# A block's first projection with the high-half passes ahead of the low-half passes, and the wait for the low half between them

## The chip, the cores and the metric

The kernel runs on one core of a Trainium2 chip. The metric is the device time of the whole program in microseconds (us). Engines are named as in the profile: PE is TensorE (PEld its weight loads), DVE is VectorE, ACT is ScalarE, POOL is GpSimd, SP issues the DMAs.

## The reference

Two layers, each over 2048 prompt rows and 32 sample rows of width 1024. A layer normalises its input, projects it once for all head groups, runs sparse attention (A), a gated linear recurrence (B) and retention (C), gates each group and projects back. Cut to what matters:

```python
def mixer_layer(x, pos, k_past, v_past, ik_past, s_hgrn, s_ret, lb, norm_g, w_in, ...):
    h = rms_norm(x, norm_g)
    proj = jnp.einsum('btd,dn->btn', h, w_in)
    (aq, ak, av, ag, iq, ik, iw, bq, bf, bi, bg, cq, ck, cv, cg) = jnp.split(proj, SPLIT_IDX, axis=-1)
    aq = rope(rms_norm(aq.reshape(b, t, A_HEADS, HEAD_DIM), q_norm_g), pos)
    ...
    ya = sparse_attention(aq, iq, iw * IDX_W_SCALE, pos, k_all, v_all, ik_all) * jax.nn.silu(ag)
    ...
    s_hgrn_new, ob = chunked_scan(gla_chunk, ...)
    ...
    s_ret_new, oc = chunked_scan(ret_chunk, s_ret.astype(f32), (cq, ck, cv))
    ...
    y = jnp.concatenate([ya, yb.astype(ya.dtype), yc.astype(ya.dtype)], axis=-1)
    out = x + jnp.einsum('btm,md->btd', y, w_out)
```

The change touches the `proj` product alone. It is computed in near-f32 precision from f16 halves: h = high + low, w = high + low, and the sum high x high + high x low + low x high is accumulated in f32.

## The kernel before

**Layers.** Each layer has two halves, one after the other. `recurrent_half` normalises and projects the rows, runs both recurrences, and writes queries, keys and gates to DRAM. `attention_half` reads them back, searches the top keys, attends and projects out. In between all engines meet.

**Blocks.** The recurrent half walks over 17 blocks of rows: blocks 0 to 15 of 128 prompt rows, and block 16 with the 32 sample rows. Block 0 is written out, blocks 1 to 14 are a hardware loop of seven passes with two blocks in each, and blocks 15 and 16 are written out again. Every engine has its own program in this form, so each has a back edge after blocks 2, 4, ..., 12. What one engine needs of another it waits for by semaphore, in the fixed order of its own program.

**The projection.** The 3912 output columns are eight groups in the order `bqf`, `big`, `cqk`, `cvg`, `iq`, `kvi`, `aq`, `ag` (`GI` is a group's place in it, 0 for `bqf`). `project` (L345) computes one group into one bank of PSUM (`PJ`, four banks in turn): for each of the `DC` = 8 chunks of 128 input columns, three matmuls, with the transposed input as stationary operand and 512 columns of weights as the moving one. L362 is high input by high weights, L363 high input by low weights, L364 low input by high weights. That is 24 matmuls for a group and 192 for a block.

**Where the input comes from.** The transposed input of block t + 1 is made during block t. ACT rounds the normalised rows to f16 (`xh`), DVE takes the remainder (`xl`, L840). In the middle of the last group `ag` of block t, after 5 of its 8 chunks, PE transposes both (`x_transposes`, L342) into two PSUM banks. ACT copies the first bank to `hTh` (L483, semaphore `hTh_ok`), and DVE copies the second to `hTl` (L845, semaphore `hTl_ok`). Nine matmuls of `ag` are still to come on PE then. DVE's copy stands in its program behind the norm of `aq`: L813 and L815 on `sqa`, of which L813 waits for POOL's `rsa`. ACT has only the gate of `ag` behind its copy.

**The start of a block.** PE's `block_of` waits for both semaphores, then projects `bqf`, transposes the rotated queries of the block before (`qrp`, which DVE finishes at L650), projects `big`, and transposes `bqf`, which ACT has copied. From these ACT makes `ef` (L503), and DVE's work on the new block begins with it at L699. Ahead of that DVE still ends the old block: the rotation of `aq` into `qrp`, the output of retention, the gate `ga`, and `ql`, the low half of the queries (L831).

**Block 0** has one thing more to wait for: the f16 halves of the weights. ACT rounds them (`w_in_hi`, L470), and DVE (L854) and, for three chunks in each of the groups 2 to 6, POOL (L610, L612) make the low halves (`w_in_lo`). At `t == 0` every `project` waits for all low weights of its group (L359).

Of the kernel before, what the change touches and what calls it, by code (L numbers as in the profile page):

```python
# [75 lines left out]
def build(nc, xin, cache_k, cache_v, cache_i, st_h, st_r, norm_g, w_in, q_g, k_g, lb_logits, h_g, r_g, w_out,  # L76
# [3 lines left out]
    DC = D // P  # L80
# [24 lines left out]
    def recurrent_half(l, sem):  # L105

        with ExitStack() as ctx:
            def sb(name, shape, dt=F32):
                return ctx.enter_context(nc.sbuf_tensor(f"{name}_{l}", shape, dt))


            wh, wl = sb("w_in_hi", [P, DC * N_IN], F16), sb("w_in_lo", [P, DC * N_IN], F16)
# [13 lines left out]
            hTh, hTl = sb("hTh", [P, 2, DC, P], F16), sb("hTl", [P, 2, DC, P], F16)  # L126
# [33 lines left out]
            def ps(name):  # L160
# [14 lines left out]
            x_sq, x_ms, x_rs, xh_ok, xl_ok, xT_ok, hTh_ok, hTl_ok = (sem(n) for n in (  # L175
                "x_sq", "x_ms", "x_rs", "xh_ok", "xl_ok", "xT_ok", "hTh_ok", "hTl_ok"))
# [21 lines left out]
            def weights(g, c, half):  # L198

                n0, wd = DC * GOFF[GROUPS[g][0]] + c * GROUPS[g][1], GROUPS[g][1]  # L200
                return half[:, n0:n0 + wd]
# [125 lines left out]
            def _(pe):  # L327
                mm = nc.tensor.matmul
# [16 lines left out]
                def project(t, T, par, n, c0=0, c1=DC):  # L345

                    g = GI[n]
                    wd = GROUPS[g][1]
                    if c0 > 0:
                        pass  # L350
                    elif not isinstance(t, int) or t > 0 or g >= PJ_BANKS:
                        pn = GROUPS[(g - PJ_BANKS) % NG][0]
                        tt = t if g >= PJ_BANKS else t - 1
                        if pn in ACT_G:
                            pe.wait_ge(act_read, tt * len(ACT_G) + ACT_G[pn])
                        if pn in DVE_G:
                            pe.wait_ge(dve_read, tt * len(DVE_G) + DVE_G[pn])
                    if isinstance(t, int) and t == 0:
                        pe.wait_ge(w_lo_ok[g], DC)  # L359
                    out = PJ[g % PJ_BANKS][0:T, 0:wd]  # L360
                    for c in range(c0, c1):
                        mm(out, hTh[:, par, c, 0:T], weights(g, c, wh), start=(c == 0), stop=False)  # L362
                        mm(out, hTh[:, par, c, 0:T], weights(g, c, wl), start=False, stop=False)  # L363
                        last = mm(out, hTl[:, par, c, 0:T], weights(g, c, wh), start=False, stop=(c == DC - 1))  # L364
                    if c1 == DC:
                        last.then_inc(proj, 1)

                def block_of(t, T, par):
                    pe.wait_ge(hTh_ok, t + 1)
                    pe.wait_ge(hTl_ok, t + 1)  # L370
                    project(t, T, par, "bqf")
                    if not isinstance(t, int) or t > 0:
                        query_transposes(t - 1, P)
                    project(t, T, par, "big")
                    pe.wait_ge(act_read, t * len(ACT_G) + ACT_G["bqf"])
                    transposes(trv[0], [bqf[0:T, c, :] for c in range(4)], T).then_inc(bqfT_ok, 1)
                    project(t, T, par, "cqk")
                    project(t, T, par, "cvg")
                    project(t, T, par, "iq")
# [5 lines left out]
                    for p in range(2):  # L385
                        last = nc.tensor.transpose(TR[0][0:T, p * P:(p + 1) * P], k2T[:, p, 0:T], ident[:])
# [4 lines left out]
                    for p in range(2):  # L391
                        for i in reversed(range(T // WIN)):
                            m = (WIN, 2 * WIN, P, P)[i]
                            q = qe if i == 0 else qw
                            for h in range(2):
                                r = slice(64 * h, 64 * h + 64)
                                last = mm((ATT, OU)[h][0:m, p * P + i * WIN:p * P + (i + 1) * WIN], kt[r, p, i, 0:m],
                                          q[r, p, i * WIN:(i + 1) * WIN], start=True, stop=True)
# [9 lines left out]
                    for p in range(2):  # L408
                        for h in range(2):
                            r = slice(64 * h, 64 * h + 64)  # L410
                            last = mm((ATT, TR[0])[h][0:T, p * P:p * P + T], cqkT[r, 2 + p, 0:T], cqkT[r, p, 0:T],
                                      start=True, stop=True)
# [10 lines left out]
                    for c, s in enumerate((akh[:, 0:P], akh[:, P:2 * P], akl[:, 0:P], akl[:, P:2 * P])):  # L423
                        last = nc.tensor.transpose(trh[0][:, c, 0:T], s[0:T, :], identh[0:T, 0:T])
# [23 lines left out]
                pe.wait_ge(prep, 1)  # L448
                x_transposes(0)
                block_of(0, P, 0)  # L450
                if NB > 2:
                    with pe.Fori(1, NB - 1, 2) as t:
                        block_of(t, P, 1)
                        block_of(t + 1, P, 0)
# [1191 lines left out]
    with ExitStack() as whole:  # L1646
        def sem(name):
            return whole.enter_context(nc.semaphore(name))
# [151 lines left out]
```

## Time and profile before

| | us |
|---|---|
| median of 3 runs | 4125.5 (4125.13 to 4126.38) |
| the profiled execution | 4124.83 |
| its span in the trace | 4123.0 |
| recurrent half, layer 0 / layer 1: first matmul | 14.0 / 2072.1 |
| attention half, layer 0 / layer 1: first matmul | 940.3 / 2998.5 |
| PE busy over the span | 3622.0 (88%) |
| DVE / ACT / POOL busy | 2644.5 / 2336.1 / 1070.5 |
| L362, L363, L364: matmuls each | 2176 |

The three lines of `project` are the dearest on PE, 814 + 812 + 811 us by the sum of their durations. A matmul of 512 columns lasts about 0.38 us in the records and the next one begins about 0.22 us after it, so they overlap, and what a stream of them costs is read from the starts. A row of the order of time names in brackets how long the engine was idle before it and which instruction released it.

### The profile page before, as it was taken

To read this page: it belongs to the slowest core of one execution; us is meant where nothing else is said; L and a number is where in the kernel's file an instruction comes from. 1 tells how busy PE (TensorE), PEld (TensorE's weight loads), DVE (VectorE), ACT (ScalarE), POOL (GpSimd) and SP (SyncE) were. 2 spreads that over 40 slices of the span, in tenths; PEclk is the share of its full clock that TensorE was granted. 3 is DMA by queue.
4 is the path that set the end of the run, shared out by engine and by line. 5 is a ranking of instruction groups with operands and counts; after the bars stand their busy time and mean duration, and the time that the engine had idled before them with its cause. 6 is when DMAs were issued, how large, how long until landed. Compare 5 with 4: busy or idle time off the path is not lost. (4 is left out here: it accounts for less than half of the span.)

```text
span 4123.0 us, 57079 instructions
## 1 busy us (share of the span) xinstructions
PE 3622.0 (88%) x17620; PEld 1694.0 (41%) x17620; DVE 2644.5 (64%) x6138; ACT 2336.1 (57%) x4386; POOL 1070.5 (26%) x1772
## 2 busy tenths in 40 slices
PE   5999999985888889889859999999858888898897
PEld 2555555541333323243325555555413333233443
DVE  6666666656676766656266666666566767666562
ACT  5333333326779888777253333333267798887772
POOL 4110010004533332333040001010055333323330
PEclk8999999996889999989979999999968899999899
DMA  5111111115200000001151111111152000000010
GB/s 179 37 39 37 37 37 40 38 28 145 80 33 32 21 22 26 15 28 35 37 178 39 37 36 37 39 38 38 27 144 82 30 33 21 22 26 15 28 35 38
DMA packets 168514, 194.54 MB, mean 47 GB/s; under 512 B 76576, under 2 KB 114464, under 8 KB 168288
## 3 DMA queue, kind: packets, MB, share of 16 engines
q1 hardware_dynamic: 168288, 192.01, 15.2%
q8 instruction: 83, 1.36, 0.1%
q14 instruction: 143, 1.17, 0.1%
HBM read 130.57 MB, written 61.36 MB: 47 GB/s over the span
## 5 line engine op out<-in xcount | busy, mean ns | idle before, releaser
L1441 ACT ACTIVATE signs<-sc,mid 128x640 bf16<-128x640 f32 (+14 forms) x720 | 974.8, 1355 | 251.7 <-POOL mid L1497 234.7
L362 PE MATMUL PJ<-w_in_hi,hTh 128*128 128x512 f16 (+2 forms) x2176 | 813.8, 374 | 69.6 <-DVE hTl L845 34.7
L363 PE MATMUL PJ<-w_in_lo,hTh 128*128 128x512 f16 (+2 forms) x2176 | 812.3, 373 | 0.0
L364 PE MATMUL PJ<-w_in_hi,hTl 128*128 128x512 f16 (+2 forms) x2176 | 811.1, 373 | 0.0
L1346 PE MATMUL PV<-pt,va_p 128*65 128x512 f32 x1088 | 583.8, 624 | 77.2 <-ACT pt L1421 71.0
L1589 DVE SCALAR_TENSOR_TENSOR sc<-rl,iwb,sc 128x512 f32<-128x512 f32 (+5 forms) x602 | 416.3, 709 | 287.3 <-ACT rl L1412 279.2
L1494 POOL TENSOR_SCALAR dlt<-cnta,stp 128x1 f32<-128x1 f32 (+1 forms) x720 | 274.5, 381 | 1137.4 <-ACT signs L1441 1135.5
L1497 POOL TENSOR_SCALAR mid<-mid,dlt,stp 128x1 f32<-128x1 f32 (+1 forms) x720 | 434.8, 604 | 75.6
L1526 DVE CUSTOM_DVE_ANT_0 junkb<-AX,mneg 128x512 bf16<-128x512 f32 (+5 forms) x720 | 412.3, 601 | 39.6 <-PE AX L1291 32.5
L1421 ACT ACTIVATE pt<-LG 128x512 f32<-128x512 f32 (+1 forms) x612 | 330.6, 554 | 141.7 <-PE LG L1331 123.6
L1412 ACT ACTIVATE rl<-AX 128x512 f32<-128x512 f32 (+5 forms) x688 | 345.3, 530 | 105.9 <-PE AX L1304 79.6
L362 PEld LDWEIGHTS PJ<-w_in_hi,hTh 128*128 128x128 f16 (+1 forms) x2176 | 214.4, 99 | 305.7 <-issue 73.8
L364 PEld LDWEIGHTS PJ<-w_in_hi,hTl 128*128 128x128 f16 (+1 forms) x2176 | 214.8, 99 | 241.3 <-issue 7.5
L1303 PE MATMUL AX<-key2h_p,iq 128*128 128x512 f16 (+3 forms) x608 | 238.8, 396 | 79.0 <-ACT rl L1412 59.9
L363 PEld LDWEIGHTS PJ<-w_in_lo,hTh 128*128 128x128 f16 (+1 forms) x2176 | 214.6, 99 | 211.5 <-issue 5.5
L596 POOL TENSOR_TENSOR rsx<-ssx,mhalf 128x1 f32<-128x1 f32 x34 | 19.0, 558 | 958.5 <-DVE ssx L835 958.5
L1304 PE MATMUL AX<-key2l_p,iq 128*128 128x512 f16 (+3 forms) x608 | 238.0, 395 | 0.0
L1331 PE MATMUL LG<-identb,mneg 128*128 128x512 bf16 (+1 forms) x612 | 237.2, 388 | 0.0
L1346 PEld LDWEIGHTS PV<-pt,va_p 128*65 128x65 f32 x1088 | 144.7, 142 | 219.1 <-ACT pt L1421 96.3
L1384 PE MATMUL X<-w_out_hi,yTh 128*128 128x512 f16 (+1 forms) x544 | 208.9, 384 | 11.3 <-DVE yTl L1564 7.4
L1572 DVE SCALAR_TENSOR_TENSOR xr<-X,xr 128x512 f32<-128x512 f32 (+1 forms) x68 | 46.9, 690 | 261.3 <-PE X L1386 261.2
L1385 PE MATMUL X<-w_out_lo,yTh 128*128 128x512 f16 (+1 forms) x544 | 208.6, 384 | 0.0
(268 smaller groups left out, 5885.9 us busy)
## 6 DMA issues: line engine op xcount, KB each, us to landing
yt<-y_d SPq DMA_DIRECT2D x32, 512.0 KB, 3.5
out<-xr SPq DMA_DIRECT2D x32, 512.0 KB, 2.6
w_in_hi<-in SPq DMA_DIRECT2D x40, 256.0 KB, 4.9
w_stage<-in SPq DMA_DIRECT2D x40, 256.0 KB, 3.9
x<-in SPq DMA_DIRECT2D x16, 512.0 KB, 3.8
w_in_lo<-in SPq DMA_DIRECT2D x32, 256.0 KB, 6.4
y_d<-ga SPq DMA_DIRECT2D x32, 256.0 KB, 2.0
q<-q_d SPq DMA_DIRECT2D x32, 256.0 KB, 2.8
```

What stands on the lines that cost most here:

```text
L362: mm(out, hTh[:, par, c, 0:T], weights(g, c, wh), start=(c == 0), stop=False)
L363: mm(out, hTh[:, par, c, 0:T], weights(g, c, wl), start=False, stop=False)
L364: last = mm(out, hTl[:, par, c, 0:T], weights(g, c, wh), start=False, stop=(c == DC - 1))
L1303: mm(ps[0:T, 0:wd], q, keys[c][2][0][:, c0:c0 + wd], start=True, stop=False)
L1346: mm(PV[0:HD + 1, 0:4 * T], va[c][0:kw, k0 // P, kv, :], pt[0:kw, (n - 1) % 3, 0:4 * T], start=(k0 == 0), stop=(k0 + kw == keys_of(j)[1])) ...
L1412: A(rl[0:T, (n - 1) % 3, 0:wd], ax_bank("idx", j, k)[0:T, 0:wd], ACT.Relu).then_inc(s["relu_ok"], 1)
L1421: A(pt[0:kw, (n - 1) % 3, 0:4 * T], LG[(n - 1) % 3][0:kw, 0:4 * T], ACT.Exp, scale=HD ** -0.5).then_inc(s["exp_ok"], 1)
L1441: A(signs[p][0:T, 0:W], sc[u % 3][0:T, 0:W], ACT.Sign, scale=-1.0, bias=small[u % 3]["mid"][0:T, :], accum_out=small[u % 3]["cnta"][0:T, : ...
L1494: G.tensor_scalar(v["dlt"], v["cnta"], float(W - 2 * K), stp[0:T, u % 3, i:i + 1], ALU.is_le, ALU.mult).then_inc(s[f"dlt_ok{p}"], 1)
L1497: G.tensor_scalar(v["mid"], v["mid"], v["dlt"], stp[0:T, u % 3, i + 1:i + 2], ALU.add, ALU.subtract).then_inc(s[f"mid_ok{p}"], 1)
L1526: V.tensor_tensor_reduce(out=junk[0:T, n % 2, 0:wd], in0=ax_bank("qk", j, k)[0:T, 0:wd], in1=mneg[j % 3][0:T, c0:c0 + wd], scale=1.0, scal ...
L1589: V.scalar_tensor_tensor(out=o, in0=src, scalar=w1, in1=o, op0=ALU.mult, op1=ALU.add).then_inc(s["acc_ok"], 1)
```

## The change

Group 0 (`bqf`) alone is affected. Its loop over the chunks now has the two passes with `hTh` only; after it comes the wait for `hTl_ok`, and then the eight passes with `hTl` in a loop of their own. The wait for `hTl_ok` at the head of `block_of` is gone. The other seven groups keep their three passes chunk by chunk.

```diff
@@ -361,13 +361,17 @@
                     for c in range(c0, c1):
                         mm(out, hTh[:, par, c, 0:T], weights(g, c, wh), start=(c == 0), stop=False)
                         mm(out, hTh[:, par, c, 0:T], weights(g, c, wl), start=False, stop=False)
-                        last = mm(out, hTl[:, par, c, 0:T], weights(g, c, wh), start=False, stop=(c == DC - 1))
+                        if g > 0:
+                            last = mm(out, hTl[:, par, c, 0:T], weights(g, c, wh), start=False, stop=(c == DC - 1))
+                    if g == 0:
+                        pe.wait_ge(hTl_ok, t + 1)
+                        for c in range(DC):
+                            last = mm(out, hTl[:, par, c, 0:T], weights(g, c, wh), start=False, stop=(c == DC - 1))
                     if c1 == DC:
                         last.then_inc(proj, 1)
 
                 def block_of(t, T, par):
                     pe.wait_ge(hTh_ok, t + 1)
-                    pe.wait_ge(hTl_ok, t + 1)
                     project(t, T, par, "bqf")
```

On PE, at the back edge of the loop, before (the end of `ag` of one block, the branch, and `bqf` of the next; names in brackets are the semaphores waited for):

```order
L364 MATMUL PJ_0<-w_in_hi,hTl 128x512
L452 REGISTER_ALU
L452 COMPARE_AND_BRANCH
L362 MATMUL PJ_0<-w_in_hi,hTh 128x512 [waits dve_read,hTl_ok,hTh_ok]
L363 MATMUL PJ_0<-w_in_lo,hTh 128x512
L364 MATMUL PJ_0<-w_in_hi,hTl 128x512
...
L333 MATMUL ATT<-ident,qrp 128x128 [waits aq_ok]
```

and the same place now (L365 is what was L364 in the groups after the first, L369 the new loop, L456 the old L452):

```order
L365 MATMUL PJ_0<-w_in_hi,hTl 128x512
L456 REGISTER_ALU
L456 COMPARE_AND_BRANCH
L362 MATMUL PJ_0<-w_in_hi,hTh 128x512 [waits dve_read,hTh_ok]
L363 MATMUL PJ_0<-w_in_lo,hTh 128x512
...
L369 MATMUL PJ_0<-w_in_hi,hTl 128x512 [waits hTl_ok]
L369 MATMUL PJ_0<-w_in_hi,hTl 128x512 x7
L333 MATMUL ATT<-ident,qrp 128x128 [waits aq_ok]
```

The wait for `hTl_ok` moved from the first of the 24 matmuls to the 17th, and the eight matmuls that read `hTl` moved behind the sixteen that don't.

On PE, in block 0, before (the transposes of x, then `bqf`):

```order
L342 MATMUL TR_0<-identh,xl 128x128 [waits xl_ok]
L342 MATMUL TR_0<-identh,xl 128x128 x7
L362 MATMUL PJ_0<-w_in_hi,hTh 128x512 [waits w_lo_ok0,hTl_ok,hTh_ok]
...
L362 MATMUL PJ_0<-w_in_hi,hTh 128x512 [waits w_lo_ok1]
```

and now:

```order
L342 MATMUL TR_0<-identh,xl 128x128 [waits xl_ok]
L342 MATMUL TR_0<-identh,xl 128x128 x7
L362 MATMUL PJ_0<-w_in_hi,hTh 128x512 [waits w_lo_ok0,hTh_ok]
...
L369 MATMUL PJ_0<-w_in_hi,hTl 128x512 [waits hTl_ok]
L369 MATMUL PJ_0<-w_in_hi,hTl 128x512 x7
L362 MATMUL PJ_0<-w_in_hi,hTh 128x512 [waits w_lo_ok1]
```

The wait for the low weights of group 0 stays at the head; the one for those of group 1 (`w_lo_ok1`, at `big`) stays where it was.

## Rows read from the trace of the kernel before

**Rows 1.** Costliest groups: line, engine, operation, count | busy, mean ns | idle before, releaser.

```profile
L362 PE MATMUL PJ<-w_in_hi,hTh 128*128 128x512 f16 (+2 forms) x2176 | 813.8, 374 | 69.6 <-DVE hTl L845 34.7
```

**Rows 2.** By stretch: stretch, length, busy PE, PEld, DVE, ACT, POOL; clock, DMA share, GB/s.

```profile
71.00:900.00 829.00, 797.04 (x4855) 448.06 (x4856) 555.19 (x1380) 278.32 (x652) 88.17 (x87) 0.99 0.14 40
```

**Rows 3.** Waits of PE, 117 to 910, then 2177 to 2970: total, times, longest.

```profile
PE PJ L362 <- DVE hTl L845: 12.8, 14, 0.9
PE PJ L362 <- issue: 1.2, 2, 0.8
...
PE PJ L362 <- DVE hTl L845: 12.0, 13, 0.9
```

**Rows 4.** Order of time, start of block 3: start, duration, instruction [idle before <-releaser].

```profile
214.94 0.61 PE L342 MATMUL TR<-identh,xl 128*128 128x128 f16 x8
215.14 1.02 ACT L483 ACTIVATE hTh<-TR 128x1024 f16<-128x1024 f16 x1 [1.15 <-PE TR L342]
...
217.12 0.38 PE L364 MATMUL PJ<-w_in_hi,hTl 128*128 128x512 f16 x1
...
217.47 0.69 DVE L845 COPY hTl<-TR 128x1024 f16<-128x1024 f16 x1
...
218.42 0.39 PE L362 MATMUL PJ<-w_in_hi,hTh 128*128 128x512 f16 x1 [0.92 <-DVE hTl L845]
```

**Rows 5.** Order of time: start of block 16 in layer 0, of block 1 in layer 1.

```profile
869.96 0.69 DVE L845 COPY hTl<-TR 128x1024 f16<-128x1024 f16 x1
...
870.75 0.38 PE L362 MATMUL PJ<-w_in_hi,hTh 128*32 128x512 f16 x1 [0.46 <-issue]
...
2175.92 0.69 DVE L845 COPY hTl<-TR 128x1024 f16<-128x1024 f16 x1 [0.47 <-PE TR L342]
...
2177.03 0.38 PE L364 MATMUL PJ<-w_in_hi,hTl 128*128 128x512 f16 x1
...
2177.24 0.38 PE L362 MATMUL PJ<-w_in_hi,hTh 128*128 128x512 f16 x1
```

**Rows 6.** Order of time behind the start of block 3; then DVE's waits, 117 to 900.

```profile
220.18 0.42 DVE L650 TENSOR_TENSOR qrp<-rt 128x256 f32<-128x256 f32 x1
...
223.60 0.60 PE L333 MATMUL ATT<-ident,qrp 128*128 128x128 f32 x4
...
227.90 0.69 DVE L831 TENSOR_TENSOR ql<-ATT,qh 128x512 f16<-128x512 f32 x1 [3.67 <-issue]
...
230.48 0.30 DVE L699 TENSOR_SCALAR ef<-ef 128x256 f32<-128x256 f32 x1 [1.89 <-ACT ef L503]
...
DVE ef L699 <- ACT ef L503: 58.9, 16, 4.8
...
DVE ql L831 <- issue: 21.1, 6, 3.7
```

**Rows 7.** Order of time, block 0 of layer 0.

```profile
17.77 2.73 DVE L854 SCALAR_TENSOR_TENSOR w_in_lo<-w_in_lo,ng,w_in_hi 128x512 f16<-128x512 f32 x4
...
21.21 0.58 PE L362 MATMUL PJ<-w_in_hi,hTh 128*128 128x512 f16 x1 [4.91 <-DVE hTl L845]
...
29.13 0.39 PE L362 MATMUL PJ<-w_in_hi,hTh 128*128 128x512 f16 x1 [0.33 <-DVE w_in_lo L854]
...
48.82 0.42 ACT L512 ACTIVATE qe<-bT 128x256 f32<-128x256 f32 x1 [5.20 <-DVE qw L723]
...
53.93 1.56 POOL L610 TENSOR_SCALAR w_in_lo<-w_in_lo,ng 128x512 f32<-128x512 f32 x1 [3.89 <-ACT w_in_hi L470]
```

**Rows 8.** Instruction queues by packets, MB and share: 110 to 218; then 218 to 821.

```profile
q8 instruction: 5, 0.08, 0.3%
...
q14 instruction: 32, 0.26, 0.1%
```

**Rows 9.** By stretch, from the first matmul of each attention half on.

```profile
940.33:2047.00 1106.67, 956.78 (x3690) 372.74 (x3691) 696.15 (x1561) 844.84 (x1454) 408.88 (x761) 0.91 0.14 42
2998.46:4105.00 1106.54, 956.74 (x3689) 372.77 (x3690) 695.92 (x1561) 844.94 (x1454) 408.99 (x761) 0.91 0.14 43
```

## The prediction

> **What bounds the kernel now.** I read the costliest groups first, then the busy time of each engine by stretch, then the waits of PE alone in the block loops, then the order of time around one block start, and last the rows behind it on DVE.
>
> The group of L362 is the dearest matmul line, and the largest part of the idle time ahead of it is put down to `hTl`, 34.7 us [rows 1]. By stretch, PE is busy for 797.04 of the 829 us from 71 to 900, DVE for 555.19 and ACT for 278.32, with a granted clock of 0.99 [rows 2]; in the attention half behind it PE is busy for 956.78 of 1106.67 us at a clock of 0.91 [rows 9]. So the recurrent half is PE's. Its waits from block 1 on are short: 12.8 us in 14 waits for `hTl` and 1.2 us in 2 waits under "issue" in layer 0, 12.0 us in 13 waits and again 1.2 us in 2 in layer 1, and nothing else [rows 3]. Nothing else means that an interval taken out of PE here shortens the stage, unless another engine is met first.
>
> One start shows what it is, that of block 3 [rows 4]. PE transposes the low half of x at 214.94. ACT copies `hTh` from 215.14 for 1.02 us: ready at 216.16. DVE copies `hTl` only from 217.47, since the work on `sqa` stands ahead of it, for 0.69 us: ready at 218.16. PE's last matmul of `ag` begins at 217.12 and the next at 218.42. Without a wait one of these matmuls follows the last after 0.21 us, as in layer 1 from 2177.03 to 2177.24 [rows 5]. So 1.30 - 0.21 = 1.09 us is lost, and `hTh` is ready 1.2 us before PE could use it.
>
> **The change part by part.** *Removed: the wait for `hTl` at a block's head.* The idle number of a row leaves out that a waiting matmul also no longer overlaps the end of the last one: 0.38 us for one against a pitch of 0.21, 0.17 us more. Blocks 1 to 16 of both layers: 12.8 + 12.0 + 2 x 1.2 = 27.2 us idle over 14 + 13 + 4 = 31 starts, plus 31 x 0.17 = 5.3: **32.5 us**. The two "issue" waits of each layer belong in it. They are the starts of blocks 15 and 16, which stand outside the loop: at block 16 DVE's copy ends at 869.96 + 0.69 = 870.65 and PE goes at 870.75 after 0.46 us idle [rows 5], so it is the same wait under another name. The 32nd start is block 1 of layer 1: `hTl` was done at 2176.61, the matmul came at 2177.24 with no idle time [rows 5], nothing to gain.
>
> *Put in its place: the same wait 16 matmuls later.* PE now stands only for `hTh`, 1.2 us early. The 16 matmuls cover 16 x 0.21 = 3.4 us, from about 217.33 to 220.7, and `hTl` is there at 218.16. The new wait costs nothing while `hTl` is less than 3.4 us behind the end of `ag`; today it is 0.83. Behind this wait stand the 8 low matmuls, the transposes of `qrp` and the projection `big`, and none is held. The wait instruction itself adds nothing either: the head of block 1 in layer 1 holds the same waits, met, and the pitch there is the plain 0.21 us. Count and kind of the matmuls, weight loads, DMAs and the work of the other engines are unchanged: 0. SP's queue, POOL and ACT are moved past nothing.
>
> *What is late next.* PE comes 1.09 us earlier against what DVE still has to do of the old block. The first such meeting is `qrp`: DVE ends it at 220.60, PE wants it at 223.60, then at 222.5 [rows 6]; 1.9 us of slack stay. The second is on DVE's side: it waits 1.89 us for `ef`, which PE's transposes release, and this is its tightest start, since `ql` ahead of it came late, after 3.67 us under "issue" [rows 6]. After the change 0.8 us of that wait are left (the mean of the 16 waits is 58.9 / 16 = 3.7, and the longest 4.8). So DVE is still the one that waits, falls in with PE at `ef` in each block, and its `hTl` keeps its place relative to PE. The gain therefore repeats in every block rather than being used up once.
>
> *The first block of each layer* loses 4.9 us to `hTl`, but I book 0. The low weights, which DVE makes before `hTl`, are ready at 20.5 (17.77 + 2.73), so PE could start at 20.5 instead of 21.21 [rows 7], 0.7 us. Then `big` waits for DVE's next low weights at 29.13 in any case, and that was DVE's pace, not PE's [rows 7]. ACT's early copy of `bqf` lets POOL start up to 0.7 us earlier, but POOL stands 3.89 us for ACT before 53.93, and ACT stands 5.20 us for DVE before 48.82 [rows 7], which is DVE's chain from `big` on. The bounds are 0 and 2 x 0.7 = 1.4 us; I take 0, by these waits.
>
> *A price that the trace of before can't show* is a stall of PE's own at a loop's back edge, now under the wait. There are 6 back edges in each layer, and the stall lies between 0 and 1.09 us. DVE pays such a one: 3.67 us, 6 times. For PE I take 0, by the instruction queues: from 110 to 218 two of them carry packets, from 218 to 821 only q14 is left, with 32 packets, though PE runs six more passes of its loop [rows 8]. What PE runs from 218 on is thus no longer fetched; the q14 packets go with DVE's stalls. The Trainium skill (Runtime: NRT & Kernel Launch, "Instruction fetch mechanics") says that a taken branch whose target isn't in the fetched stretch stalls until a DMA has brought it. By that rule the 12 back edges would give nothing and the gain would be 19.4 us. The same section gives PE a larger instruction memory than the others, which agrees with the empty queue.
>
> *The attention halves* only start earlier. Their two passes are alike: PE's busy time is 956.78 and 956.74 us, at a clock of 0.91 in both [rows 9]. The three timed runs differ by 1.25 us, so I allow 1.3 us either way.
>
> Sum: 4124.83 (profiled execution; span 4123.0) - 32.5 = 4092.3. The median of the runs is 0.7 above that execution: **4093.0 us**.
>
> **The rivals.** *A, the back edges stall* (the mechanism above). For it: DVE's 3.67 us. Against it: the empty queue. 12 x 1.09 = 13.1 us stay: 4093.0 + 13.1 = 4106.1.
>
> *B, DVE becomes the bound.* DVE is busy for two thirds of the stage (555.19 of 829 us, [rows 2]), but in chains with POOL and ACT; if one reaches from block to block without touching PE, shortening PE only moves the wait to `qrp` or to the first use of DVE's output. For it: DVE's waits for PE are the only slack, and 1.89 us is the least of them. Against it: 1.89 is more than 1.09, and it is the shortest of the `ef` waits. If it held in full the gain would be 0: 4125.5, no change.
>
> *C, slower: the clock in the attention halves.* There PE falls to the low level (1.2 of 2.4 GHz) whenever it has stood idle for a while, and 0.91 over 1106 us is 2 x 0.09 x 1106 = 199 us at that level in each [rows 9]. The two halves would now begin 14.0 + 16 x 0.17 = 16.7 and 32.5 us earlier, with idle times placed differently against the moments at which the level changes. A microsecond more at the low level costs up to 0.5 us. To end over 8.3 us slower, 32.5 + 8.3 = 40.8 us would have to be lost, 82 us more at the low level in the two halves, a clock of 0.89 in place of 0.91. A clock of 0.885 means 2213 x 0.05 = 111 us more at that level, and 4093 + 55 = 4148. Against it: the two halves and the three runs agree to within 1.3 us, whatever their start. The Trainium skill (TensorE: Matmul & The Clock Gate, "What you observe") has the moment of the rise vary by half a microsecond from run to run; no row here shows that apart.
>
> *D, the change doesn't do what it says*: in the built order the new wait might stand at the head again. The order shows it at the 17th matmul; no chance of its own.
>
> **How the numbers follow.** Forecast 0.88 (4093.0), A 0.05 (4106.1), B 0.04 (4125.5), C 0.03 (4148). The forecast's own range is 1.4 (first blocks) + 1.3 below and 1.3 above, with half of A's loss (6.5 us) as the bound of the unknown back edge: 4090 to 4101. It leaves out 0.12 and a little of the forecast's own edges, so it is also the range. This kernel's measurement can tell about 0.2%, 8.3 us, from no change. Faster by more: 0.88 + 0.05 = 0.93; within: 0.04; slower: 0.03.
>
> **What would show it.** The waits of PE from block 1 on have no row for `hTl` and none under "issue", and a block takes 49.1 us instead of (870.75 - 218.42) / 13 = 50.2. The first matmul of L362 comes 0.21 us after the last of `ag`. DVE's wait for `ef` falls by 1.1 us, to 0.8 at the least. `big` of block 0 still begins near 29.1, behind a longer wait for `w_in_lo`. The first matmul of L369 shows no idle time outside block 0. An idle time at every second block's start would be A; waits for `qrp` or for other work of DVE would be B; 0.89 or less over an attention half would be C. The forecast is wrong if the block's period stays above 49.6 us.

## The result, and the profile of the changed kernel

| us | before | after |
|---|---|---|
| median of 4 runs each, on one chip | 4125.94 (4125.13 to 4126.95) | 4099.51 (4098.27 to 4103.01) |
| the profiled execution | 4124.83 | 4098.27 |
| its span | 4123.0 | 4096.5 |
| first matmul of the program | 14.0 | 13.6 |
| recurrent half, layer 0: first matmul to first of the attention half | 926.3 | 914.0 |
| attention half, layer 0: first matmul to first of layer 1 | 1131.8 | 1134.8 |
| recurrent half, layer 1 | 926.3 | 908.4 |
| attention half, layer 1, to the end | 1124.5 | 1125.7 |

After over before is 0.9938, with a 95% interval of 0.9923 to 0.9952: the medians are 26.4 us apart, some 0.6% faster. That is inside the predicted range, of the predicted sign, and 6.5 us short of the predicted 4093.0. The two recurrent halves gave 12.3 and 17.9 us, the first matmul came 0.4 us earlier, and the attention halves, which the change doesn't touch, took 3.0 and 1.1 us back.

The wait is gone. Of the costliest groups, the line that answers to [rows 1] is:

```profile
L362 PE MATMUL PJ<-w_in_hi,hTh 128*128 128x512 f16 (+2 forms) x2176 | 814.2, 374 | 41.6 <-POOL w_in_lo L616 30.4
```

The idle time ahead of L362 fell from 69.6 to 41.6 us, and what is left is mostly block 0's wait for POOL's low weights. By stretch, the row that answers to [rows 2] has PE busy for 808.31 us where it was 797.04:

```profile
71.00:900.00 829.00, 808.31 (x4945) 456.03 (x4945) 564.74 (x1412) 280.48 (x660) 90.31 (x90) 0.99 0.14 40
```

The waits of PE from block 1 on in layer 0 (total, times, longest; [rows 3] before):

```profile
PE TR L333 <- DVE cks L748: 1.8, 6, 0.5
PE ATT L333 <- DVE qrp L654: 1.5, 1, 1.5
```

Nothing waits for `hTl` or stands under "issue". Layer 1 has the second line alone, which is block 16's and not new: the kernel before has the same 1.5 us at 918.68, behind the end of the window of [rows 3]. The first line is new: six waits for `cks`, DVE's scaled copy of the rotated `bqf`, in layer 0 only.

The start of block 3, in order of time ([rows 4] before):

```profile
214.08 1.02 ACT L487 ACTIVATE hTh<-TR 128x1024 f16<-128x1024 f16 x1 [1.14 <-PE TR L342]
...
216.05 0.38 PE L365 MATMUL PJ<-w_in_hi,hTl 128*128 128x512 f16 x1
...
216.27 0.38 PE L362 MATMUL PJ<-w_in_hi,hTh 128*128 128x512 f16 x1
...
216.41 0.69 DVE L849 COPY hTl<-TR 128x1024 f16<-128x1024 f16 x1
```

The last matmul of `ag` begins at 216.05, the first of `bqf` 0.22 us later across the back edge, while DVE's copy of `hTl` has not even begun. It ends at 217.10, and the passes that need it come from about 219.7 on. All as forecast. Measured between the transposes of x, a block takes 49.07 us (it was about 50.2) in layer 1 and in most of layer 0; only the first of the fifteen is 0.1 us longer. In layer 0 the six blocks behind a back edge take 49.57 to 49.88 instead, 3.8 us more in all.

### The profile page after: what moved, and what is told of

Its sections match the earlier page's. It is cut to its first block and busy times, and to the rows that moved or that the text cites. A ratio compares the mean times of both kernels' runs of the same rounds, so it can differ in the third digit from the quotient of the medians.

```text
span 4096.5 us, 56951 instructions
## 1 busy us (share of the span) xinstructions
PE 3606.4 (88%) x17520; PEld 1693.7 (41%) x17620; DVE 2642.2 (65%) x6138; ACT 2335.4 (57%) x4386; POOL 1073.1 (26%) x1772
## 5 line engine op out<-in xcount | busy, mean ns | idle before, releaser
L362 PE MATMUL PJ<-w_in_hi,hTh 128*128 128x512 f16 (+2 forms) x2176 | 814.2, 374 | 41.6 <-POOL w_in_lo L616 30.4
L365 PE MATMUL PJ<-w_in_hi,hTl 128*128 128x512 f16 (+3 forms) x1904 | 706.7, 371 | 0.0
L1425 ACT ACTIVATE pt<-LG 128x512 f32<-128x512 f32 (+1 forms) x612 | 330.5, 554 | 141.1 <-PE LG L1335 98.9
L362 PEld LDWEIGHTS PJ<-w_in_hi,hTh 128*128 128x128 f16 (+1 forms) x2176 | 214.6, 99 | 268.0 <-issue 27.5
L365 PEld LDWEIGHTS PJ<-w_in_hi,hTl 128*128 128x128 f16 (+1 forms) x1904 | 187.7, 99 | 208.1 <-issue 6.3
L1390 PE MATMUL X<-w_out_hi,yTl 128*128 128x512 f16 (+1 forms) x544 | 209.0, 384 | 0.0
```

The source lines that it names most:

```text
L1425: A(pt[0:kw, (n - 1) % 3, 0:4 * T], LG[(n - 1) % 3][0:kw, 0:4 * T], ACT.Exp, scale=HD ** -0.5).then_inc(s["exp_ok"], 1)
```

## The experiments

Ratios are against the kernel before, run on the same chip beside it; medians of different experiments come in part from different chips, so ratios and the blocks in the traces are what to compare. "Blocks" is the time of the fifteen blocks between the transposes of x for block 1 and those for block 16, worked out from the trace; before it is 752.9 in layer 0 and 751.4 in layer 1, after it is 740.0 and 736.3.

### The changed kernel again

No edit.

> The changed kernel once more, unaltered. Theory: 4098 to 4103 us again; blocks 1 to 16 of the recurrent halves gain the same 13.6 and 15.8 us in every execution, and what differs from run to run (some 5 us) lies in block 0 of each layer and in the first 250 us of each attention half, where the granted clock changes level at other moments. Rival: the blocks themselves vary, then the block period of 49.07 us isn't met again.

Median 4098.8 (5 runs), ratio 0.9934 (0.9920 to 0.9947). Blocks 741.5 and 736.3, again six waits for `cks`, 1.8 us in all. The shortfall of layer 0 against layer 1 repeats. The blocks themselves did vary a little, against the expectation: one period of layer 0 was 51.49 us here, where the same block took 49.73 in the first trace. It is the clock. A stretch of this period, in front of which PE had waited 0.45 us for `cks` and then run short matmuls of 32 columns, was granted the low level (length, busy times, clock third from the end):

```profile
444.90:448.30 3.40, 3.40 (x17) 1.89 (x16) 2.73 (x11) 0.00 (x0) 0.56 (x1) 0.50 0.00 0
```

3.4 us at half the clock make 1.7 us of the 2.4 by which this period is over 49.07; the other 0.7 is what the back edges cost elsewhere too. The other five waits for `cks` of this layer had no such stretch behind them; what decides was not tested.

### The new order of passes with the wait left at the head

```diff
                     if g == 0:
-                        pe.wait_ge(hTl_ok, t + 1)
                         for c in range(DC):
...
                 def block_of(t, T, par):
                     pe.wait_ge(hTh_ok, t + 1)
+                    pe.wait_ge(hTl_ok, t + 1)
```

> The passes of the first projection in the new order, but the wait for hTl at the head again. Theory (the gain is the wait's place alone): the time of the kernel before, 4125.5 us, and the starts of the blocks wait 0.93 us for hTl as before. Rival (the order of the matmuls saves or costs by itself): another time; 4099 if all of the gain were the order's.

Median 4125.04 (10 runs), ratio 0.9997 (0.9988 to 1.0007): no change. Blocks 752.9 and 751.4. Its waits of PE are those of before:

```profile
PE PJ L362 <- DVE hTl L849: 12.7, 14, 0.9
PE PJ L362 <- issue: 1.2, 2, 0.8
```

So the order of the passes is worth nothing by itself. The gain is the place of the wait. The two waits under "issue" went with it in the changed kernel and came back here, so they are waits for `hTl` under another name, as forecast.

### The copy of hTl earlier on DVE, the kernel otherwise as before

```diff
                     V.tensor_tensor(iql[:, :, 0:T], trv[1][:, :, 0:T], iqh[:, :, 0:T], ALU.subtract).then_inc(iql_ok, 1)
+                    if T == P:
+                        hT_low(t + 1, 1 - par)
                     dve.wait_ge(rsa_ok, t + 1)
...
-                    if T == P:
-                        hT_low(t + 1, 1 - par)
                     dve.wait_ge(iqT_ok, t + 1)
```

> The kernel before with the copy of hTl moved on DVE ahead of the norm of aq (L813, L815), into the time in which DVE waits for POOL's rsa; PE's program unchanged. Theory (the price at a block's head is only hTl's lateness behind L813 and L815): hTl is ready at about 0.7 us after the transposes, before PE ends ag, PE waits for nothing there, a block takes 49.07 us, and the time is that of the changed kernel, 4096 to 4100. Rival (DVE pays for it: rsa's consumers 0.4 us later make PE wait elsewhere): waits for qrp or cks, 4105 or more.

Median 4090.94 (4 runs), ratio 0.9913 (0.9897 to 0.9928), 5 us under the expected 4096; blocks 737.6 and 736.9. PE waits for neither `hTl` nor `cks`; block 16's `qrp` alone is left:

```profile
PE ATT L333 <- DVE qrp L650: 1.5, 1, 1.5
```

Removing the lateness at its source gives at least what the change gives: 2.4 us more in layer 0's blocks, where DVE still fetches code in every pass (32 instruction packets from 218 to 800; see below), and 0.7 less in layer 1's. So the blocks give 1.7 us more than those of the changed kernel. The rest of the difference in time lies in stretches that no edit touched.

### The copy of hTl later on DVE, with the old and with the new order

The same edit to both kernels:

```diff
-                    if T == P:
-                        hT_low(t + 1, 1 - par)
                     dve.wait_ge(iqT_ok, t + 1)
                     rotate(step, t, T, sqa[0:T, :], qrp[0:T, :], 8, (), (aq_ok, t + 1))
+                    if T == P:
+                        hT_low(t + 1, 1 - par)
```

> The kernel before with the copy of hTl moved on DVE behind the rotation of aq, 2.5 us later. Theory: PE's wait at a block's head grows from 0.93 to 3.4 us, 2.5 us more in 31 or 32 blocks, some 4203 us. Rival: DVE's earlier qrp gives some of it back, 4180.

> The changed kernel with the same late copy of hTl. Theory (16 matmuls cover 3.45 us): the copy ends 3.3 us after the end of ag, right at the edge; PE waits 0 to 0.1 us at the first matmul of L369, the time is that of the changed kernel plus 0 to 3.5 us, 4098 to 4103. Rival (the wait in the middle of a group costs something by itself, or covers less): several tenths of a us in each block, 4110 or more.

With the old order: 4251.21 (2 runs), ratio 1.0302 (1.0283 to 1.0321). PE waits 3.5 us at every start, in layer 0:

```profile
PE PJ L362 <- DVE hTl L845: 48.0, 14, 3.5
```

2.6 us more per start than before would give about 4207, near the expected 4203, and 44 us more are lost. They are the clock's. Most blocks now take 54.4 us, a few 52.7. Two windows of about one block each (length, busy times, clock third from the end), and PE in order of time behind one such wait:

```profile
379.00:434.00 55.00, 51.52 (x307) 28.41 (x306) 34.58 (x89) 16.87 (x40) 5.33 (x6) 0.97 0.12 35
488.00:540.00 52.00, 48.52 (x300) 27.36 (x299) 33.46 (x82) 16.87 (x40) 4.46 (x5) 1.00 0.12 35
```

```profile
391.72 0.39 PE L362 MATMUL PJ<-w_in_hi,hTh 128*128 128x512 f16 x1 [3.48 <-DVE hTl L845]
...
393.62 0.63 PE L363 MATMUL PJ<-w_in_lo,hTh 128*128 128x512 f16 x1
394.05 0.63 PE L364 MATMUL PJ<-w_in_hi,hTl 128*128 128x512 f16 x1
...
396.44 0.38 PE L364 MATMUL PJ<-w_in_hi,hTl 128*128 128x512 f16 x1
```

After 3.48 us idle the matmuls start 0.22 us apart for about a microsecond, then 0.43 apart (0.63 long, the 1.2 GHz level) for 3.4 us, and then 0.22 apart again. That costs 1.7 us, the difference between the two kinds of block. The trace has 13 such stretches in the blocks of layer 0 and 12 in those of layer 1, which makes some 42 of the 44 us.

With the new order: 4103.31 (4 runs), ratio 0.9943 (0.9927 to 0.9958), at the upper end of the expected 4098 to 4103. The same copy is as late, and PE passes over it in layer 1 without a wait (blocks 736.2). Block 3 of layer 0:

```profile
219.84 0.69 DVE L849 COPY hTl<-TR 128x1024 f16<-128x1024 f16 x1
...
220.38 0.38 PE L363 MATMUL PJ<-w_in_lo,hTh 128*128 128x512 f16 x1
...
220.60 1.90 PE L369 MATMUL PJ<-w_in_hi,hTl 128*128 128x512 f16 x8
```

The copy ends at 220.53 and the first low pass begins at 220.60 with no idle time, 3.46 us after the first of the 16 matmuls (217.14): their cover is real to its full length. In layer 0 the blocks take 746.3 us, 10 more than in layer 1, and DVE's lateness shows at `cks`:

```profile
PE TR L333 <- DVE cks L748: 5.4, 6, 1.0
```

With 0.17 each for the lost overlap these six waits make 6.4 of the 10 us. Most of the rest is the clock again: from 247.6 to 251.0 and from 647.0 to 650.4 the granted clock was 0.50, and the two blocks that hold these stretches took 51.8 and 52.0 us where the other four behind a back edge took 50.0 to 50.3.

### Where DVE's loop lies in the instruction memory

In layer 0 DVE pauses once per pass for 3.7 us ahead of `ql`, and in layer 1 never, though the instructions are the same, before and after the change. A few memsets of one column each are hardly work; what they do is move the loop. The edit puts `A` of them ahead of DVE's loop in layer 0 and `B` behind its last block there, and leaves the rest of the changed kernel as it is:

```diff
                 block_of(0, P, 0)
+                for i in range(A if l == 0 else 0):
+                    V.memset(pad[:, i:i + 1], 0.0)
                 if NB > 2:
...
                 query_low(NB, TS)
+                for i in range(B if l == 0 else 0):
+                    V.memset(pad[:, i:i + 1], 0.0)
```

A = 10, B = 118:

> The changed kernel with 10 tiny memsets on DVE ahead of its loop in layer 0 and 118 after the last block of that layer, where DVE waits for the DMAs; they only move where DVE's loop lies in its program, by 10 instructions in layer 0 and by 128 in layer 1. Theory (DVE's 3.66 us under issue at 6 back edges of layer 0 is fetching of its code, which layer 1 with another place of the loop doesn't have, and it makes PE wait for cks): those stalls go, the waits of PE for cks between 117 and 910 go from 1.8 us to 0, every block takes 49.07 us, and the time is some 3.8 us under that of the changed kernel, 4094 to 4097. Rival (the loop itself costs 3.66 us in layer 0, or DVE's chain is simply too long): no change in waits, the same time.

Median 4091.27 (5 runs), ratio 0.9922 (0.9908 to 0.9935). Layer 0 now is like layer 1: blocks 736.2 and 736.3, every period from the second on 49.07 or 49.08 us, and no wait of PE at all between 117 and 900. The median is under the expected 4094 to 4097, for the blocks gave the 3.8 us expected of them and other stretches gave more (below). The instruction packets of queue `q14`, 218 to 800 us, in the changed kernel and then in this one:

```profile
q14 instruction: 32, 0.26, 0.1%
```

```profile
q14 instruction: 2, 0.02, 0.0%
```

So 30 of the 32 packets, five in each of six passes, go with the place of DVE's loop; the two that are left come with either. Ten instructions stand ahead of the loop of layer 0, and its blocks became 3.8 us faster. All four traces with them have 736.2 us there; the five traces of the changed kernel without them, with `hTl` copied where it was, have 739.8 to 741.5. B = 118 was to keep layer 1's loop off a bad place; that loop is without pauses with it and without it. The profiled execution, 4091.27, is 7.0 us below that of the changed kernel: 3.8 in the blocks of layer 0, 0.7 in its block 0, and 2.9 behind block 15 of layer 0, where nothing was edited but the 118 memsets, less 0.4 for a later first matmul. The 3.8 are shown; the rest is no more than what such stretches vary by (below).

A = 0, B = 112, meant to bring the pauses into layer 1:

> The changed kernel with 112 tiny memsets on DVE after the last block of layer 0, nothing ahead of its loop. Theory: layer 0 keeps its six stalls, and DVE's loop in layer 1 now lies as layer 0's does, so layer 1 gets six stalls of 3.66 us too and PE waits there for cks; the time is some 3.8 us over that of the changed kernel, about 4103. Rival: layer 1 stays free of them, same time.

The expected pauses did not come: blocks 739.8 and 736.6, no pauses in layer 1, median 4096.81 (5 runs), ratio 0.9935 (0.9921 to 0.9948). From the packets' start times, DVE's fetches in its first pass here came when it was at instructions 0, 133 and 261 of the loop; in layer 0, with the pauses, at 4, 137 and 261. (One more packet of `q14` comes in the first pass of layer 0, near instruction 181, with pauses and without.) B = 106 was to bring layer 1 to the latter:

> The changed kernel with 106 tiny memsets on DVE after the last block of layer 0 instead of 112. In the runs so far DVE's code is fetched again on every pass where the fetches of the first pass came 4, 137 and 261 instructions into the loop, and not where they came at -1, 129 and 255 (10 memsets) or 0, 133 and 261 (112 in layer 1). Theory (a few instructions decide, by where the loop begins in its fetched piece): 106 put layer 1's at about 6, so layer 1 gets six stalls of 3.66 us on DVE, PE waits for cks at 6 blocks, and the blocks of layer 1 take 3 to 4 us longer than 736.25. Rival: layer 1 stays at 736.3 to 736.6.

Median 4098.75 (4 runs), ratio 0.9937 (0.9922 to 0.9952). The fetches of layer 1 came at 4, 139 and 263, the six pauses are there, and `q14` has 32 packets from 2260 to 2850 us, where the changed kernel has 2. DVE's waits in layer 1 (the second row is of `ef` for its own first step), then PE's:

```profile
DVE ql L836 <- issue: 21.1, 6, 3.6
...
DVE ef L705 <- DVE ef L704: 3.6, 6, 0.8
```

```profile
PE TR L334 <- DVE cks L749: 0.3, 2, 0.2
```

Layer 1's blocks went from 736.3 to 737.9, 1.7 us instead of the 3 to 4 expected. So the pauses come and go with the loop's place, and what they cost PE differs between the layers. The trace shows why. One back edge stalls DVE at a second place too, where the next piece of code begins (shown below, at the step that failed). In layer 0 that is ahead of `ef`, and the stall makes DVE 0.76 to 1.07 us late. Here the piece begins two instructions later, behind the first step of `ef` (L704): that step starts as soon as ACT is done, the stall follows it, and it makes DVE only 0.42 to 0.76 us late. That is the second row, whose six waits would be 0.03 us each without it.

### Block 0 in its old order, blocks 1 to 16 in the new

```diff
-                        if g > 0:
+                        if g > 0 or (isinstance(t, int) and t == 0):
                             last = mm(out, hTl[:, par, c, 0:T], weights(g, c, wh), start=False, stop=(c == DC - 1))
-                    if g == 0:
+                    if g == 0 and not (isinstance(t, int) and t == 0):
...
                     pe.wait_ge(hTh_ok, t + 1)
+                    if isinstance(t, int) and t == 0:
+                        pe.wait_ge(hTl_ok, 1)
```

> The changed kernel with block 0 of each layer in the order of before, with its wait for hTl at the head. Theory (in block 0 the early start gains nothing, and the longer idle time ahead of big lets the granted clock fall there in layer 0): block 0 of layer 0 takes 99.3 us as in the kernel before instead of 100 to 101.5, ahead of big PE waits 0.3 us instead of 2 us, and the time is 1 to 1.5 us under the changed kernel's. Rival (block 0 differs from run to run only): no difference.

> The changed kernel with the memsets and with block 0 in the order of before. Theory (block 0 differs from run to run by the moments at which the clock changes level, not by the order): block 0 of layer 0 takes 99 to 101.5 us as in all the other runs, and the time is that of the memsets alone, 4091 give or take 3. Rival (the new order costs block 0 1.3 us): 1.3 us less, reliably 99.3.

The second is this edit on top of A = 10, B = 118. Medians 4094.22 (5 runs) and 4093.90 (5 runs), ratios 0.9932 (0.9919 to 0.9946) and 0.9923 (0.9909 to 0.9936). The first, beside 4099.51, looks as if the new order cost block 0 something. But block 0 took 99.8 and 98.9 us in it, and 100.9 and 101.4 in the second; in the changed kernel 100.5 and 98.9, and before the change 99.2 and 101.2. It lies between 98.6 and 101.6 in all fourteen traces, with either order. Ahead of `big` PE waited 1.2 and 0.5 us in the two, where 0.3 was expected (0.33 before, 1.98 in the changed kernel). The medians with the loop moved, 4091.27 without the edit and 4093.90 with it, go the other way. What the order does to block 0 is smaller than what varies it, and isn't resolved.

### All of it together

Two more: the kernel before with the early copy and A = 10, B = 118, and the changed kernel with both.

> The kernel before with the early copy of hTl and the memsets, PE's program unchanged. Theory: 736.2 to 737 us for the blocks of each layer, the same time as with the changed order and the memsets, 4090 to 4094.

> Everything together: the changed order on PE, the early copy of hTl on DVE, and the 10 and 118 memsets. Theory (the two cures of the wait for hTl are alternatives, the memsets cure something else): 736.2 us for the blocks of both layers as with the memsets alone, 4090 to 4093. Rival: the early copy gives something of its own, 4088 or less.

Medians 4091.42 (4 runs) and 4090.82 (5 runs), ratios 0.9913 (0.9898 to 0.9928) and 0.9917 (0.9904 to 0.9931); blocks 736.2 and 736.9 in both. The early copy, the moved loop, and both with either order all end at 4091, some 8 us below the changed kernel and 35 below the kernel before, and are not told apart. Of the 8 us their blocks show 1.7 (the early copy alone), 3.8 (the moved loop alone) or 3.1 (both); the rest has no cause that the runs show, and the 95% intervals of all four reach into that of the changed kernel. So the early copy with the unmoved loop is shown to be as good as the change, and not more than that. The simplest of them is the early copy alone, which moves one call of the kernel before.

## Why the prediction was right, and where it was short

**Right in the mechanism, and in the range by luck of its upper bound.** The wait went, PE ran on, and the gain came back in every block: that is what was forecast. But 4099.51 lies in the range only because its upper end had been moved out by 6.5 us for a stall of PE's own at its back edges, and that stall measured nothing. What was missing came from two things that the sum had at 0: a stall of DVE's (3.8 us) and longer attention halves (4.1 us). Block 0 and the first matmul gave 1.4 back.

**The main term held.** The forecast took 32.5 us out of the starts of blocks 1 to 16. The blocks gave 13.0 + 15.2 (752.9 - 740.0 and 751.4 - 736.3, before rounding), and from there to the attention half, with the start of block 16 in it, another 0.57 and 0.53: 29.2. With the 3.8 us added back that the six slow periods of layer 0 cost, it is 33.0. Period 49.07, no row for `hTl`, no idle time at L369 outside block 0: as written.

**The step that failed: "0.8 us of that wait are left".** [Rows 6] show DVE waiting 1.89 us for `ef` in block 3, behind 3.67 us under "issue" at `ql`. The prediction reads the 1.89 as slack against PE. In the changed kernel, the same place:

```profile
226.82 0.69 DVE L835 TENSOR_TENSOR ql<-ATT,qh 128x512 f16<-128x512 f32 x1 [3.66 <-issue]
...
227.81 0.39 ACT L507 ACTIVATE ef<-TR 128x256 f32<-128x256 f32 x1
...
229.18 0.29 DVE L703 TENSOR_SCALAR ef<-ef 128x256 f32<-128x256 f32 x1 [1.66 <-ACT ef L507]
```

ACT has `ef` ready at 228.20 and DVE begins 0.98 us later. The bracket names ACT, but ACT isn't what DVE waited for last. The trace also holds each instruction packet's start and the register and branch instructions, which the rows leave out. The first packet comes 1.6 us after DVE's branch back to the start of its loop, which runs at 224.34 before and at 223.28 after; `ql` is the first work behind that branch. One register instruction stands between `ql` and `ef` and waits for nothing. Worked out from them:

| us | before | after |
|---|---|---|
| first packet of `q14` starts | 226.00 | 224.93 |
| `ql` starts | 227.90 | 226.82 |
| second packet starts | 228.68 | 227.37 |
| the register instruction behind `ql` | 230.38 | 229.08 |
| ACT's `ef` is ready | 230.36 | 228.20 |
| DVE's `ef` starts | 230.48 | 229.18 |

Both packets are followed by the next instruction after 1.7 to 1.9 us. The register instruction, which had nothing to wait for, came only with the second piece of code: at 230.38 before, 0.02 us behind ACT's `ef`. So the 1.89 us were not slack against PE. They were taken up by the fetch of that piece, which happened to end together with ACT's `ef`:

```profile
229.97 0.39 ACT L503 ACTIVATE ef<-TR 128x256 f32<-128x256 f32 x1
```

Of the six back-edge blocks this is the tightest; in the others DVE's register instruction came 0.1 to 0.4 us ahead of ACT's end. With 1.09 us taken out of PE the piece is the later one in all six: DVE's `ef` starts 0.8 to 1.1 us behind ACT's end, where 0.03 is usual. With the loop moved both go: the same register instruction runs 0.03 us after `ql` starts, and the row of DVE's waits for `ef` holds all 16 and ACT alone:

```profile
DVE ef L704 <- ACT ef L508: 66.8, 16, 4.7
```

The forecast's other sign, that DVE's wait for `ef` falls by 1.1 us in each block, was also off. DVE's waits in the changed kernel, 117 to 900, and one row of them before:

```profile
DVE ef L703 <- ACT ef L507: 52.1, 15, 4.7
...
DVE ql L835 <- ACT qh L578: 0.4, 1, 0.4
...
DVE ef L703 <- issue: 2.0, 1, 2.0
```

```profile
DVE ql L831 <- ACT qh L574: 7.6, 10, 0.9
```

For `ef` the sum fell from 58.9 to 54.1 us, 0.3 per wait; as much again and more, 7.2 us, came out of the wait for `qh` ahead of `ql`. In a block without a fetch DVE had slack in both places, so nothing was lost by it there.

**What was late next** followed from that. DVE stays late from `ef` on through the norm of `k2T` and the rotation of `bqf`, and PE meets it at `cks`:

```profile
243.08 0.42 DVE L748 TENSOR_TENSOR cks<-bqf,ksc 128x256 f32<-128x256 f32 x1
...
243.56 0.66 PE L333 MATMUL TR<-ident,bqf 128*128 128x128 f32 x4 [0.35 <-DVE cks L748]
```

Six such waits hold 1.8 us, with 0.17 each for the lost overlap 2.8; the periods show 3.8. A row leaves out that the transposes behind such a wait also start a little further apart. Block by block the trace fits one relation: the period is longer by DVE's lateness behind `ef` less 0.27 us. (Lateness is the time from ACT's end to the start of DVE's second step on `ef`, over the 0.36 us that it takes elsewhere.) For the six blocks of layer 0 the lateness is 0.94, 0.79, 0.92, 0.76, 1.07 and 0.92 us, 5.4 in all, less 1.6: the 3.8. It holds to 0.02 us in 35 of the 36 blocks behind a fetching back edge in the five traces of the changed order with an unmoved copy (the 36th is the one with the low clock), the cheaper pauses of layer 1 with B = 106 among them (3.4 less 1.6, where the blocks show 1.7). Rival B named the mechanism (PE waits at another first use of DVE's output) but took it for the whole of both layers. It was six blocks of one layer, and behind a code fetch.

**Rival A had the right kind of price on the wrong engine, and the wrong size.** PE's own back edge costs nothing, as the head of block 3 shows. The fetch at a back edge that the change uncovered was DVE's, which the prediction set aside with the words that the `q14` packets "go with DVE's stalls": true, and there was a second one under the first. It cost 3.8 us; rival A had put 13.1 on PE's. The Trainium skill (Runtime: NRT & Kernel Launch, "Instruction fetch mechanics") has a taken branch stall when its target isn't in the fetched stretch. The trace agrees for DVE in layer 0, whose first work behind the branch stands 3.67 us; in layer 1 the same instructions do not stall.

**Block 0, booked at 0**, came out at +1.3 and -2.2 us in the two layers, -1.0 in all. Its first matmul and its wait at `big` are as read from [rows 7]:

```profile
20.21 0.59 PE L362 MATMUL PJ<-w_in_hi,hTh 128*128 128x512 f16 x1 [4.36 <-DVE w_in_lo L858]
...
28.93 0.39 PE L362 MATMUL PJ<-w_in_hi,hTh 128*128 128x512 f16 x1 [1.98 <-DVE w_in_lo L858]
```

`bqf` begins 1.0 us earlier (0.45 of that before the first matmul of the program) and `big` only 0.2 us earlier, so the gain is lost at `w_in_lo` as forecast. Block 0 varies by up to 3 us from trace to trace with either order.

**The attention halves, booked at 0 and 1.3 either way**, gave back 3.0 and 1.1. That is three times the allowance, and where it could be traced the mechanism is that of rival C in small. One place holds 2.5 of the 3.0. Before and after, the stretch between the same two `rl` of ACT in the attention half of layer 0:

```profile
1048.95:1071.00 22.05, 16.12 (x67) 6.61 (x66) 17.61 (x41) 12.06 (x23) 15.91 (x26) 0.92 0.43 131
```

```profile
1036.26:1060.80 24.54, 18.38 (x67) 7.39 (x66) 17.55 (x41) 12.11 (x23) 16.85 (x26) 0.79 0.38 121
```

67 matmuls in both, at a clock of 0.92 and of 0.79. The output projection in it begins, before and after, with:

```profile
1065.14 0.39 PE L1384 MATMUL X<-w_out_hi,yTh 128*128 128x512 f16 x1 [2.31 <-DVE yTl L1564]
1065.36 0.38 PE L1385 MATMUL X<-w_out_lo,yTh 128*128 128x512 f16 x1
```

```profile
1052.68 0.61 PE L1388 MATMUL X<-w_out_hi,yTh 128*128 128x512 f16 x1 [1.86 <-DVE yTl L1568]
1053.08 0.63 PE L1389 MATMUL X<-w_out_lo,yTh 128*128 128x512 f16 x1
```

After a similar idle time (2.31 and 1.86 us) the same matmuls run at the high level before and at the low one after, until 1057.3. The shorter idle time is the one followed by the slower matmuls, so its length doesn't decide it; what does was not tested. Such moments differ from kernel to kernel and from run to run. Leaving out the late copy with the old order, the stretch behind block 15 of layer 0 took 1202.7 to 1208.4 us over the traces and the last one of layer 1 1192.8 to 1199.0, with nothing of the attention halves edited; and the kernel before, beside the experiments, ran between 4119.5 and 4130.6. The allowance was taken from three runs within 1.3 us of each other, which was too few. By these spreads it should have been some 5 us.

**The sum:** 33.0 (starts) - 3.8 (DVE's second fetch) + 1.0 (block 0) + 0.4 (first matmul) - 4.1 (attention halves, of which the clock is shown for 2.5) = 26.5, and 26.5 in the spans.

## What to carry to other kernels

A wait that a profile puts down to another engine gives an upper bound of your slack, not its size: compare the end of the named releaser with the start that it released, and look hardest right behind an "issue" gap, where a second code fetch can hide. When an interval is taken out of the engine that bounds a stage, see which loops of the others fetch code in each pass (instruction packets per pass), since a few instructions more or less ahead of a loop can switch that off or on. Moving a late copy forward on its producer did as much here as reordering its consumer.

## What the hardware showed that I had not expected

- Whether DVE fetches its loop again in every pass hangs on where the loop lies, to within a few instructions. With first-pass fetches at its instructions 4, 137 and 261 (and 4, 139, 263 in the other layer) there were six pauses of 3.6 us and 32 packets; with -1, 129 and 255 none and 2 packets. At 0, 133 and 261 there were none either (layer 1 of A = 0, B = 112). The count tells how far DVE had come when the packet started, and not at which instruction a piece begins: in layer 0 of the late copy with the old order, where DVE stood idle ahead of `ql` when the first packet came, it was about 2, and there were fetches in every pass. So the exact boundary is open.
- At such a back edge three pieces of 8 KB come one after the other, 2.4 to 3.1 us from start to start, so DVE stalls at two places, 3.67 us at the first and, once PE was 1.09 us earlier, up to 1.1 us at the second. Whether the second stall lies ahead of a wait or behind it decides what it costs: 3.8 us over six blocks against 1.7.
- Ten small instructions more ahead of its loop made the blocks of layer 0 3.8 us faster.
- An idle time of PE of 3.5 us per block makes the block 5.3 us longer where the clock then falls (54.4 against 49.07) and 3.6 where it doesn't (52.7); one of 1.09 us cost only itself. But in three blocks of layer 0 (one of the changed kernel again, two of the late copy with the new order) it fell after a wait for `cks` of 0.45, 0.87 and 1.01 us, which matmuls of 32 columns had followed.
- The same 67 matmuls took 2.5 us more at a clock of 0.79 than at 0.92, in a stretch that the change doesn't touch.
